# Order of the attention jobs in the last stage of a two-layer decoder step on one Trainium2 core

## The chip, the cores and the metric

The kernel runs on one core of one Trainium2 chip. The metric is the device time of one execution in microseconds (us), as the median of several runs. The engines named below are TensorE (PE, with its weight loads as PEld), VectorE (DVE), ScalarE (ACT), GpSimd (POOL) and SyncE (SP), which only issues transfers here. All data is fp32.

## The reference

One step of a two-layer decoder for a prompt of 1024 rows (eight tiles of 128) and 32 sample rows (8 sequences of 4 tokens with a paged cache of 1024 positions). Only the second layer's attention and what follows matters here.

```
q = rope(rms(heads(q, 8), qn), pos);  k = rope(rms(heads(k, 2), kn), pos)
idx = top_k(sum_h relu(qi . ki) * wi, 256)        # per row, causal
s = q . k[idx] * 128 ** -0.5;  s = where(valid, s, -inf)
yC = (softmax(s) @ v[idx]) * silu(g_c)            # 8 heads, 2 kv heads
y = concat([yC, yX]) @ w_out                      # 1536 x 1024
out = x + y
```

The kernel doesn't gather the 256 keys. An earlier stage turns the selection into a bias for every pair of row and key. The attention then runs densely over the causal keys. A row tile i (0 to 7) so has i + 1 blocks of 128 keys.

## The kernel before

`decoder` runs the first layer, the output projection of the first layer, `layer1_front` (projections and selection of the second layer) and last `layer1_back`, the only function that the change touches.

**Jobs.** In `layer1_back` one job is one row tile and one head: 8 x 8 = 64 jobs. Job g passes through the engines in this way:

- PE `scores(g)` (L4300): q times keys, in one piece of up to 512 columns or two; tiles 4 to 7 ("long") have two pieces, tiles 0 to 3 ("short") have one. The pieces alternate between two banks, and a piece waits until DVE has read the piece two before it.
- DVE `masked(g)` (L4598): adds the bias and takes the maximum of each piece, then forms the negative maximum.
- ACT `exps(g)` (L4476).
- PE `transposes(g)` (L4312), i + 1 blocks of 128x128, and ACT `copies(g)` (L4469) out of PSUM.
- PE `mix(g)` (L4324), i + 1 products with the values, which waits until DVE has read the product of the job before.
- DVE `y_of(g)` (L4615): the product times the reciprocal sum and the gate.

**Slots.** The order of the work on each engine is written out. `back_plan` (L3785) gives 78 slots, and every engine walks them in turn; within a slot it takes the named streams one step each. Engines meet only through semaphores, so an engine can be slots ahead of another. In slot g PE does `transposes(g-3)`, `scores(g)`, `mix(g-4)`; DVE does `masked(g)`, `y_of(g-4)`; ACT does `copies(g-3)`, `exps(g)`. In the first six slots DVE takes a row preparation behind the job, in all others ahead of it.

**Row preparations.** The queries of a tile are loaded, normalised, multiplied by a gain, rotated and transposed ahead of its first job. Tiles 0 and 7 come ready from the stage before. Seven preparations remain, p = 0 to 6: tile 1, the sample rows, then tiles 6, 2, 5, 3, 4. Preparation p starts in slot `START[p]` (L3838): squares on ACT in that slot, sums on DVE in the next, `pow`, gain and rotation on POOL in the three from the next one on (p = 0: on DVE but for the `pow`), transposes on PE `TURN[p]` slots after the start. ACT then copies them over the queries of three tiles before, and waits for that tile's last scores (L4445).

**The samples.** Sixteen units (sequence, half of the cache) need four key pages each, loaded in the slots from 6 on, one unit per slot, unit u in slot u + 4 (unit 2 in slot 6). SP issues the first pages of a unit (L3988) and POOL the last one or two (L4162). PE's `smp_scores(m)` (L4228) in slots 10, 14, 18 and 22 needs the pages of units 4m to 4m + 3. Within a POOL slot the pages stand ahead of the preparation. Value pages and, from slot 37 on, slices of the output weights follow on POOL.

**Ties.** For tiles 5 and 4 a part of the selection is finished on DVE in slots 3 to 18 (`late_ties`, L4634).

**Gates.** Three buffers hold the gates of three tiles. After a tile's last job SP stores the result out of the buffer (`store_y`, five slots behind), and two slots later issues the load of the gate for the tile three further on (`load_gate`, last job + 7), which waits for the store. DVE's `y_of` waits for it (L4621).

**Weights and outputs.** From slot 45 ACT and DVE split the output weights (L4508, L4659), two slices a slot at first, and POOL loads the next slice into one of four buffers when DVE is done with it. From slot 67 PE multiplies by them, nine tiles in a row.

Of the kernel before, what the change touches and what calls it, by code (L numbers as in the profile page):

```python
# [3810 lines left out]
def job_order():  # L3811

    long, short = ([(n, h) for n in of for h in range(QH)] for of in (range(1, TILES, 2), range(0, TILES, 2)))
    return short[0:4] + [job for pair in zip(long, short[4:]) for job in pair] + long[len(short) - 4:]


def layer1_back(nc, c, a, o):
# [9 lines left out]
    rows_in = lambda t: P if t < TILES else SMP  # L3827
    cols_in = lambda t: slice(P * t, P * t + rows_in(t))
    ORDER = job_order()
    nth = lambda g: ORDER[g][0]  # L3830
    head = lambda g: ORDER[g][1]
# [3 lines left out]
    width = lambda g: (block_of(g) + 1) * P  # L3835
    halves = lambda g: [(k, min(512, width(g) - k)) for k in range(0, width(g), 512)]
    first_half = [sum(len(halves(j)) for j in range(g)) for g in range(JOBS + 1)]
    START = [0, 1, 8, 16, 24, 32, 40]  # L3838
    TURN = [7, 8, 9, 9, 9, 9, 9]
    STEPS = [[(p, s - START[p]) for p in range(PREPS) if 0 <= s - START[p] < TURN[p] + 3] for s in range(57)]  # L3840
    TURNED = lambda p: 2 * p + 1 if p else 2
# [862 lines left out]
def decoder(nc, a, o, stop=99):  # L4704
    c = Names()
    with Stage(nc, "all") as st, nc.allow_non_contiguous_dma(reason="columns of a few hundred elements"):
# [53 lines left out]
        with Stage(nc, "odd") as L:  # L4760
            index_memory(c, L)
            layer1_front(nc, c, a, o)
            if stop < 8: return
            layer1_back(nc, c, a, o)
# [57 lines left out]
```

## Time and profile before

| | us |
|---|---|
| median of 3 runs (lowest to highest) | 1782.58 (1781.74 to 1786.09) |
| profiled execution, its own time | 1781.29 |
| its span | 1779.7 |
| PE busy | 1702.0 (96%) |
| DVE busy | 960.0 (54%) |
| ACT busy | 621.0 (35%) |
| POOL busy | 424.9 (24%) |
| mean granted TensorE clock | 0.987 of full |
| stage of the jobs, first scores to last product | about 1400.7 to 1621.7 |

The span is that of the instructions. Around it lie 1.6 us more in the profiled execution. Times inside the stage are counted from the start of the span. A granted clock of 1.00 is 2.4 GHz and 0.50 is 1.2 GHz. The ends of matmuls are modelled, so durations that contain the drain of the array are read with care; a row of the chain of waits shows the part of an instruction after which the next one went on.

### The profile page before, as it was taken

How to read it: one execution, taken by the hardware profiler on the slowest of the kernel's cores; microseconds unless marked ns; L12 is line 12 of the kernel's file. 1: busy time of each engine (PE TensorE's matmuls, PEld its weight loads, DVE VectorE, ACT ScalarE, POOL GpSimd, SP SyncE). 2: the span in 40 equal slices, each digit the busy share in tenths (PEclk: the TensorE clock that was granted, in tenths of full speed). 3: DMA queues.
4: the chain of work that ended last, by engine and by line, in shares of the span. 5: the costliest groups of instructions: out<-in, count | busy, mean ns of one | idle time of the engine just before them, and what ended most of it. 6: DMA issues, size and time to landing. Idle time of an engine off the chain costs nothing. (4 is left out here: it accounts for less than half of the span.)

```text
span 1779.7 us, 26094 instructions
## 1 busy us (share of the span) xinstructions
PE 1702.0 (96%) x9141; PEld 1330.5 (75%) x9141; DVE 960.0 (54%) x2250; ACT 621.0 (35%) x1316; POOL 424.9 (24%) x665
## 2 busy tenths in 40 slices
PE   6999999999999998998999999999999599999999
PEld 5878888777788787886876566888677367777887
DVE  6724744234677665222541568888879575574111
ACT  4322332011122113110220346878856355573100
POOL 5301222100233442000362001121005665520000
PEclk9999999999999999999999999999999699999999
DMA  7433342554566467231333122334544585453231
GB/s 233 137 125 124 115 120 99 160 174 142 177 190 197 128 221 295 81 111 49 103 97 102 43 78 68 103 102 135 165 134 119 187 247 158 131 163 106 85 123 48
DMA packets 145196, 239.18 MB, mean 134 GB/s; under 512 B 21222, under 2 KB 75398, under 8 KB 145066
## 3 DMA queue, kind: packets, MB, share of 16 engines
q1 hardware_dynamic: 120650, 172.75, 30.0%
q0 software_dynamic: 18352, 57.29, 10.3%
q10 hardware_dynamic: 6064, 7.47, 1.2%
q8 instruction: 73, 1.20, 0.3%
q14 instruction: 57, 0.47, 0.1%
HBM read 171.21 MB, written 66.17 MB: 133 GB/s over the span
## 5 line engine op out<-in xcount | busy, mean ns | idle before, releaser
L1292 PE MATMUL ring_acc<-ring_w_hi,layer_xT_hi 128*128 128x512 f32 x640 | 256.6, 401 | 0.2 <-PE all_banks L1438 0.2
L1294 PE MATMUL ring_acc<-ring_w_hi,layer_xT_lo 128*128 128x512 f32 x640 | 249.8, 390 | 0.0
L1293 PE MATMUL ring_acc<-ring_w_lo,layer_xT_hi 128*128 128x512 f32 x640 | 249.7, 390 | 0.0
L2894 PE MATMUL front_acc<-front_w_hi,front_xT_hi 128*128 128x512 f32 x520 | 217.9, 419 | 9.0 <-DVE front_w_lo L3443 5.3
L2896 PE MATMUL front_acc<-front_w_hi,front_xT_lo 128*128 128x512 f32 x520 | 204.8, 394 | 0.0
L2895 PE MATMUL front_acc<-front_w_lo,front_xT_hi 128*128 128x512 f32 x520 | 204.6, 394 | 0.0
L1292 PEld LDWEIGHTS ring_acc<-ring_w_hi,layer_xT_hi 128*128 128x128 f32 x640 | 120.2, 188 | 29.8 <-issue 6.4
L1294 PEld LDWEIGHTS ring_acc<-ring_w_hi,layer_xT_lo 128*128 128x128 f32 x640 | 120.2, 188 | 26.2
L1293 PEld LDWEIGHTS ring_acc<-ring_w_lo,layer_xT_hi 128*128 128x128 f32 x640 | 120.4, 188 | 23.1
L3208 ACT ACTIVATE front_index_rows<-odd_bias,front_candidate,front_minus_sign 128x1024 bf16<-128x1024 f32 (+1 forms) x124 | 132.6, 1075 | 10.5 <-DVE front_candidate L3529 10.5
L2894 PEld LDWEIGHTS front_acc<-front_w_hi,front_xT_hi 128*128 128x128 f32 x520 | 98.2, 189 | 49.6 <-issue 18.1
L2896 PEld LDWEIGHTS front_acc<-front_w_hi,front_xT_lo 128*128 128x128 f32 x520 | 97.7, 188 | 22.5
L2895 PEld LDWEIGHTS front_acc<-front_w_lo,front_xT_hi 128*128 128x128 f32 x520 | 98.3, 189 | 16.0
L1632 ACT ACTIVATE layer_st<-ring_acc 128x512 f32<-128x512 f32 x48 | 28.7, 597 | 226.2 <-PE ring_acc L1294 226.2
L2715 POOL DMA_DIRECT2D all_w<-in_w_odd x57 | 31.9, 560 | 288.3 <-DVE front_w_lo L3443 117.9
L1115 POOL DMA_DIRECT2D all_w<-in_w_even x80 | 44.9, 563 | 216.1 <-DVE ring_w_lo L1860 105.0
L4335 PEld LDWEIGHTS all_banks<-back_v,back_first_scratch 128*128 128x128 f32 x576 | 74.2, 194 | 17.4 <-issue 12.3
L1630 ACT ACTIVATE layer_st<-ring_acc 128x512 f32<-128x512 f32 (+1 forms) x35 | 20.9, 597 | 189.5 <-PE ring_acc L1294 186.1
L4335 PE MATMUL all_banks<-back_v,back_first_scratch 128*128 128x128 f32 x576 | 76.1, 278 | 2.3 <-issue 2.3
L4607 DVE CUSTOM_DVE_ANT_0 back_first_scratch<-back_s,odd_bias 128x512 f32<-128x512 f32 (+3 forms) x96 | 51.3, 557 | 48.3 <-PE back_s L4309 47.7
L4479 ACT ACTIVATE back_first_scratch<-back_first_scratch 128x1024 f32<-128x1024 f32 (+4 forms) x64 | 49.8, 779 | 65.0 <-DVE back_first_scratch L4613 45.4
L4321 PE MATMUL all_banks<-all_ident,back_first_scratch 128*128 128x128 f32 x288 | 44.7, 283 | 8.5 <-ACT back_first_scratch L4474 5.4
(726 smaller groups left out, 3576.1 us busy)
## 6 DMA issues: line engine op xcount, KB each, us to landing
all_w<-in_w_even POOLq DMA_DIRECT2D x80, 256.0 KB, 3.9
h_even<-layer_st SPq DMA_DIRECT2D x79, 256.0 KB, 2.1
all_w<-in_w_odd POOLq DMA_DIRECT2D x61, 256.0 KB, 3.5
h_odd<-front_st SPq DMA_DIRECT2D x55, 256.0 KB, 2.1
layer_scratch<-h_even SPq DMA_DIRECT2D x46, 256.0 KB, 3.0
all_scratch<-in_w_mem SPq DMA_DIRECT2D x32, 256.0 KB, 3.2
all_scratch<-h_even SPq DMA_DIRECT2D x32, 256.0 KB, 3.6
all_scratch<-x SPq DMA_DIRECT2D x14, 512.0 KB, 3.7
```

The source lines that it names most:

```text
L1115: pool.dma_start(raw[n % RAW][:, :], a["w_even"][ORDER[chunk][0] // CW, :, CW * kk:CW * kk + CW]).then_inc(w_in[n % RAW], 16)
L1292: T.matmul(out[0:rows, :], xh[:, kk, to], wh[:, r, :], start=(kk == 0), stop=False)
L1293: T.matmul(out[0:rows, :], xh[:, kk, to], wl[:, r, :], start=False, stop=False)
L1294: ins = T.matmul(out[0:rows, :], xl[:, kk, to], wh[:, r, :], start=False, stop=(kk == KC - 1))
L2894: T.matmul(out[0:rows, :], xh[:, k, to], wh[:, r, :], start=(k == 0), stop=False, skip_group_check=True)
L2895: T.matmul(out[0:rows, :], xh[:, k, to], wl[:, r, :], start=False, stop=False, skip_group_check=True)
L2896: ins = T.matmul(out[0:rows, :], xl[:, k, to], wh[:, r, :], start=False, stop=(k == KC - 1), skip_group_check=True)
L3208: A(flags_at(i), rows_at(i), ACT.Sign, bias=cand[:, j:j + 1], scale=minus[:, j:j + 1] if k else -1.0, accum_out=cnt[:, j:j + 1]).then_inc( ...
L4321: ins = T.transpose(psT[:, 512 * j + P * q:512 * j + P * q + P], sm[g % 3][:, P * (k + q):P * (k + q) + P], c.ident[:, :])
L4335: ins = T.matmul(bankO[:, 0:P], pT[g % 2][:, k, :], v[:, k, HD * (h // 4):HD * (h // 4) + HD], start=(k == 0), stop=(k == i))
L4479: A(y, y, ACT.Exp, bias=neg[g % 3][:, :], scale=SC, accum_out=tot[g % 5][:, :]).then_inc(ex, 1)
L4607: V.tensor_tensor_reduce(sm[u][:, k:k + n], psS[:, 512 * (m % 2):512 * (m % 2) + n], c.bias[:, bias_at(i) + k:bias_at(i) + k + n], 1.0, -3 ...
```

## The change

The order of the jobs and the slots in which preparations start are changed. No instruction is added or removed.

```diff
 def job_order():
     long, short = ([(n, h) for n in of for h in range(QH)] for of in (range(1, TILES, 2), range(0, TILES, 2)))
-    return short[0:4] + [job for pair in zip(long, short[4:]) for job in pair] + long[len(short) - 4:]
+    return [job for pair in zip(short, long) for job in pair]
@@ layer1_back
-    START = [0, 1, 8, 16, 24, 32, 40]
+    START = [0, 1, 6, 14, 22, 30, 38]
     TURN = [7, 8, 9, 9, 9, 9, 9]
```

Before, jobs 0 to 3 are short, then long and short take turns from job 4 (long) to job 59 (short), and jobs 60 to 63 are long. After, even jobs are short and odd jobs long. First and last job of each tile:

| tile | 0 | 7 | 1 | 6 | 2 | 5 | 3 | 4 |
|---|---|---|---|---|---|---|---|---|
| before | 0, 11 | 4, 18 | 13, 27 | 20, 34 | 29, 43 | 36, 50 | 45, 59 | 52, 63 |
| after | 0, 14 | 1, 15 | 16, 30 | 17, 31 | 32, 46 | 33, 47 | 48, 62 | 49, 63 |

So short jobs but for the first come later, by up to three slots, and long ones earlier by three (the last four by three to none). Everything that hangs on a tile's last job (stores, gate loads) moves with it. Preparations 2 to 6 move two slots ahead on all engines and on SP, with their loads (the load for p + 2 goes out two slots behind p's transposes). The slots of the sample work, ties, weights and outputs stay.

## Rows read from the trace of the kernel before

**Rows 1.** The page: the whole span, and PE and its clock in 40 slices.
```profile
PE   6999999999999998998999999999999599999999
PEclk9999999999999999999999999999999699999999
```

**Rows 2.** By stretch: length, PE, PEld, DVE, ACT, POOL busy, granted clock, DMA share, GB/s.
```profile
1400.60:1449.00 48.40, 35.62 (x174) 23.57 (x174) 35.50 (x98) 23.67 (x70) 31.34 (x40) 0.76 0.88 270
1449.00:1476.00 27.00, 26.57 (x185) 19.51 (x189) 16.89 (x59) 14.72 (x32) 16.68 (x20) 1.00 0.77 229
1559.00:1578.00 19.00, 16.83 (x112) 13.45 (x111) 13.93 (x46) 13.30 (x29) 3.94 (x8) 1.00 0.45 145
1578.00:1612.00 34.00, 34.00 (x230) 27.54 (x229) 26.45 (x94) 26.41 (x61) 6.86 (x13) 1.00 0.54 170
```

**Rows 3.** The chain of waits from 1380 to 1450: start, us, what.
```profile
1400.01 4.39 DMA all_scratch<-h_odd
1405.51 1.23 DVE back_first_scratch L4541
1407.09 1.66 POOL back_first_scratch L4143
1410.08 1.48 DVE back_first_scratch L4541
1416.64 2.10 DVE back_first_smp L3774
1421.52 2.07 PE back_s L4309 x2
...
1436.24 1.72 PE back_s L4309 x4
1437.96 1.78 PE all_banks L4335 x16
1439.75 0.87 PE all_banks L4321 x8
```

**Rows 4.** DVE in order of time: start, us, line, operation, output and inputs.
```profile
1411.70 0.29 DVE L4607 CUSTOM_DVE_ANT_0 back_first_scratch<-back_s,odd_bias 128x128 f32<-128x128 f32 x1
...
1414.42 0.69 DVE L4607 CUSTOM_DVE_ANT_0 back_first_scratch<-back_s,odd_bias 128x512 f32<-128x512 f32 x1
...
1415.76 0.42 DVE L4613 SCALAR_TENSOR_TENSOR back_first_scratch<-back_first_scratch 128x1 f32<-128x1 f32 x1
```

**Rows 5.** PE in order of time, with its idle time and releaser in brackets.
```profile
1409.96 4.17 PE L4309 MATMUL back_s<-keys_kT,back_qT 128*128 128x512 f32 x4
...
1449.00 1.93 PE L4239 MATMUL back_x<-back_first_smp 128*32 128x512 f32 x16 [1.66 <-issue]
...
1475.90 1.92 PE L4239 MATMUL back_x<-back_first_smp 128*32 128x512 f32 x16 [0.43 <-issue]
```

**Rows 6.** POOL in order of time.
```profile
1426.30 0.79 POOL L4162 DMA_DIRECT2D back_first_smp<-in_cache_attn_kT  x1 [2.02 <-issue]
1427.49 0.73 POOL L4162 DMA_DIRECT2D back_first_smp<-in_cache_attn_kT  x1 [0.40 <-issue]
...
1433.70 1.66 POOL L4143 TENSOR_TENSOR back_first_scratch<-back_first_scratch,all_half 128x8 f32<-128x8 f32 x1 [0.89 <-DVE back_first_scratch L4542]
1435.43 2.15 POOL L4147 TENSOR_TENSOR all_scratch<-all_scratch,back_first_scratch 128x1024 f32<-128x1024 f32 x1
...
1440.68 2.37 POOL L4153 TENSOR_TENSOR all_scratch<-all_scratch 128x1024 f32<-128x1024 f32 x1
1444.25 0.74 POOL L4162 DMA_DIRECT2D back_first_smp<-in_cache_attn_kT  x1 [1.20 <-issue]
1445.02 0.47 POOL L3774 TENSOR_TENSOR all_scratch<-all_scratch 128x128 f32<-128x128 f32 x1
```

**Rows 7.** PE by stretch: length, PE busy, granted clock, DMA share, GB/s.
```profile
1381.00:1384.00 3.00, 0.21 (x1) 0.89 0.00 0
1384.00:1387.00 3.00, 2.90 (x11) 0.50 0.33 104
1387.00:1390.00 3.00, 3.00 (x8) 0.50 0.82 274
...
1447.00:1449.00 2.00, 0.34 (x4) 1.00 0.92 278
1449.00:1456.00 7.00, 7.00 (x49) 1.00 0.78 225
```

**Rows 8.** All gate loads (L3979), of their own line: time from issue to landing.
```profile
DMA to landing us min/median/max: 3.6/5.3/8.4
```

**Rows 9.** SP's own waits, 1384 to 1640: line, releaser, us in total, times, longest.
```profile
SPq L3979 <- DMA y_odd<-all_mem_vals: 4.7, 1, 4.7
```

## The prediction, made before the kernel was run

> **What bounds the kernel.** I read the page first: PE is busy in nine tenths of nearly every slice, and only slice 31 of 40 falls to 5 with the clock at 6 [rows 1]. That slice is where the changed stage begins. Busy time by stretch then divides the stage [rows 2]. From 1400.6 to 1449.0 PE is busy 35.6 of 48.4 us at a mean clock of 0.76. After that it is full but for small holes (26.6 of 27.0 us; 34.0 of 34.0 at the end) and one of 2.2 us between 1559 and 1578. So the stage is a start-up that something else bounds, and then a stretch that only the sum of PE's work bounds. The change leaves that sum alone. It can gain only by doing more PE work inside the start-up, and lose by new holes behind it.
>
> The chain of waits says what bounds the start-up [rows 3]: the load of the query rows, the sums on DVE, the `pow` on POOL, DVE again for the sample rows' sums, and the rotation that DVE makes for tile 1 (it begins at 1416.6 and ends at 1421.0). Behind it stands `masked(5)`, which releases the second piece of `scores(6)` at 1421.5. From there PE is on the chain.
>
> **Part 1, the order: what is done by slot 14.** At full clock the chain gives a long job of 8 blocks 1.72 us of scores, 1.78 of products and 0.87 of transposes [rows 3], so 0.215, 0.22 and 0.11 us a block. By the start of slot 14 the new order has done 63 blocks of scores in place of 50, 46 of transposes for 39, 45 of products for 31: 13 x 0.215 + 7 x 0.11 + 14 x 0.22 = 6.7 us more work. Before, PE stood at that point at 1447.3 (1449.0 less the idle 1.66) [rows 5]. Were all of it to fit into idle time, the gain would be 6.7 us; if none did, zero.
>
> How much fits follows from DVE. A short `masked` costs about 0.4 us and a long one 2 x 0.69 and the maximum, some 1.6 us [rows 4]. Up to slot 5 the new order has three long ones in place of one, 2.4 us more. Job 1 is now long: its scores run at the low clock, where a piece of 512 columns takes 1.0 us per record, 2.0 us a piece [rows 5], so DVE is free of it at about 1407.0, and the sums that started at 1405.5 [rows 3] start then. The whole chain of the preparation is 1.6 us late. Job 3 costs 1.2 us more, and the rotation ends near 1423.0 instead of 1421.0. But PE no longer waits for that: scores 3 and 4, the transposes of job 1 (released near 1412 by ACT) and `scores(5)` stand before it, and I find PE busy without a break from about 1417.5. It takes the product of job 1 (3.5 us at the low clock) until 1425.0. Summing slots 6 to 13 from there, with the first transposes at a mixed clock, three preparation transposes (0.6, 0.5, 0.7) and the first sample scores (1.9), I come to slot 14 at 1449.8. That is 2.5 us later with 6.7 us more done: **-4.2 us**. Bounds: -6.7 and 0.
>
> **Part 2, preparation 2 before the pages.** This costs. POOL issued its pages of units 2 to 5 first, then `pow` and gain product, then the two pages of unit 6, the second product, unit 7's page at 1444.25 and the rotation behind it [rows 6]. Unit 7's page is what `smp_scores(1)` waited for in slot 14: 4.75 us from the issue to 1449.0, 1.66 of it a hole [rows 5, 6]. Two slots ahead, all three steps of the preparation stand before unit 6. POOL's first page goes out 1.65 us later (the sample rows' `pow` hangs on the late DVE chain): 1427.9. From there, three pages at 1.15 spacing to 1431.1, `pow` and product to 1435.1, two pages behind a switch of 1.2 us to 1438.2, product to 1440.6, switch and a page to 1442.5, rotation (six of 0.45) to 1445.2, two pages, and unit 7's page at 1448.8. With the same 4.75 us the scores start at 1453.5, against PE's arrival at 1449.8: a hole of 3.7 us in place of 1.7, **+2.0 us**. Bounds: -1.7 (the page lands in time) and +3.
>
> The third preparation's steps likewise move from slots 17 to 19 to slots 15 to 17, so its rotation (2.7 us) now stands ahead of the pages of units 14 and 15, which `smp_scores(3)` needs in slot 22; that wait was 0.43 us [rows 5]. The same count puts unit 15's page at 1476.6 and its landing 3.7 us later at 1480.3, with PE there at 1478.4: a hole of 1.9, **+1.5 us**. Bounds: -0.4 and +3.
>
> **Part 3, the gates.** Tile 6's gate is issued in slot 21 and read by `y_of(17)` in slot 21; before, it was issued in slot 18 and read in slot 24. The same holds for tile 5 (slot 37) and tile 4 (slot 53). The buffer's store goes out behind `y_of(14)`; a gate load waited 4.7 us for such a store [rows 9], and lands 3.6 to 8.4 us after issue, 5.3 at the median [rows 8]. So the gate is there about 10 us after the last `y_of` of the old tile, and is wanted three slots, 8.4 us, later (19, 20 and 21 at 3.5, 1.6 and 3.3): DVE stands 1.6 us, with `masked(22)` queued behind it. PE waits for it only at `mix(18)`, behind the sample scores of slot 22, transposes and scores: 3.1 us of cover. Around slot 37 the three slots hold sample products too and last some 11 us: no stall. In slot 53 they last about 7.4 us and PE's cover is 1.4 us (transposes and scores of 5 blocks): 1.2 us at worst. I take **+0.4 us**, bounds 0 and +6.
>
> **Part 4, the weights' hole** [rows 2]. It follows from the sample rows' stores and the round of DVE, POOL, load and ACT per weight slice, tied to slots 44 to 50. There the pairs of jobs have 9 blocks in place of 10, so each pair of slots hides 0.55 us less: three pairs, less than half of them inside the hole, **+0.6 us**, bounds 0 and +1.7. The queries' copies on ACT that move two slots (each 0.6 us) stay; each now waits for scores of one slot before, not of six, and ACT's own `exps` has already waited for those: nothing. The last four long jobs become two and two; by then PE is full: **0**, bounds -0.5 and +0.3.
>
> **Sum.** -4.2 + 2.0 + 1.5 + 0.4 + 0.6 = +0.3. The profiled execution's 1781.3 becomes 1781.6; the median of the runs lay 1.3 us above it, so **1783 us**. Differences under 0.3% (5.3 us) are what a measurement of this kernel can't tell from none.
>
> **Rival 1: the pages don't hold PE.** Part 2 rests on one delay of 4.75 us from POOL's issue, in a stretch in which the DMA engines are 0.88 busy [rows 2]. If the load is lighter there or PE comes later to slot 14 than I think, the holes shrink while the gain stays: -4.2 - 1.7 - 0.4 + 1.0, so about 1777.3. For it: most pages of a unit go out on SP, whose queue the change leaves as it is. Against: the order on POOL is fixed, and 7 us of work have moved before the page.
>
> **Rival 2: the hole costs the clock too.** PE stood still for some 3 us before 1384, and the next 6 us ran at 0.50; a stop of 1.66 us at 1447 left it at 1.00 [rows 7]. The hole of 3.7 us is past the first. Six us at half clock lose 3.0 us, and PE then comes to slot 22 late enough to find its pages (-1.5): 1784.5.
> The Trainium skill (TensorE: Matmul & The Clock Gate, What's actually happening) says that the throttled state is the default and that activity lifts it; by that the loss would come with any long enough stop, and it is this rival's 1784.5 and not 1783. The rows agree in both directions.
>
> **Rival 3, slower: the gates.** If loads land as late as the slowest row, 8.4 us [rows 8], the gate comes some 13 us after the last `y_of` of the old tile. DVE then stands 4.7 us in slot 21, 2 in slot 37 and 5.7 in slot 53, and PE less its cover: 1.6 + 0 + 4.3 = 5.9 us, and two stops of DVE that long cost clock as well. It decides once landing exceeds about 7 us. Time: 1789 us. Against: the median is 5.3, and the slow rows are from the crowded start.
>
> **Chances.** The balance above 0.46; rival 1 0.20; rival 2 0.22; rival 3 0.12. Rival 1 straddles the bound: just over half of it is faster by more than 5.3 us, and nearly all of rival 3, with a little of rival 2, is slower by more. Faster 0.12, same 0.75, slower 0.13. Range 1777.5 to 1788.5: it leaves out the ends of rivals 1 and 3.
>
> **What would show it.** PE busy without a break from about 1417.5 instead of 1421.5 (part 1); POOL's `pow` of tile 6 ahead of its pages of unit 4, and PE's idle before the second sample scores near 3.7 us, with the clock behind it (part 2, rival 2); a DVE wait for a gate load in slots 21 and 53 where there was none (part 3); a weights' hole of 2.5 to 3 us. I am wrong if the first scores of job 5 come later than 1419, or if the second sample scores start without a wait.

## The result, and the profile after

The changed kernel took 1796.2 us (median; 1789.9 to 1803.2), the kernel before 1782.2 us beside it (1780.3 to 1786.1): a ratio of 1.0063, 95% interval 1.0049 to 1.0078, about 11 us slower. The medians lie 14 us apart. The runs of the changed kernel scatter by 13 us; I go by the ratio and its interval. The forecast was no change, 1783 us, and a range that ended at 1788.5. It was wrong in sign and in size.

| profiled execution, us | before | after |
|---|---|---|
| span | 1779.7 | 1795.4 |
| first scores of the changed stage | 1400.68 | 1402.44 |
| second sample scores (slot 14) | 1449.00 | 1453.10 |
| fourth sample scores (slot 22) | 1475.90 | 1482.33 |
| last sample product (slot 44) | 1557.69 | 1571.00 |
| first transposes behind the jobs (L4361) | 1621.63 | 1637.33 |

The stage itself starts between 1400.5 and 1404.8 in all profiled executions here, with either order, so the first 1.8 us are no effect of the change. From the first scores to L4361 the work is the same: 220.95 us before, 234.89 after, 13.9 us more. Behind L4361 the two agree.

The page after, PE and its clock in 40 slices, answers to [rows 1]: the slice in which the stage starts reads 6 in place of 5, and behind it two slices read 8 where before had 9.

```profile
PE   6999999999999998998999999999999698989999
PEclk9999999999999999999999999999999798999999
```

By stretch (as in [rows 2]), the start-up of the changed kernel:

```profile
1402.40:1417.50 15.10, 9.58 (x25) 4.74 (x25) 9.68 (x23) 7.44 (x15) 6.83 (x13) 0.73 1.00 303
1417.50:1440.00 22.50, 19.70 (x109) 13.66 (x113) 19.20 (x48) 10.66 (x39) 18.29 (x17) 0.84 0.87 261
1440.00:1453.10 13.10, 12.17 (x84) 8.59 (x84) 10.08 (x33) 8.61 (x19) 8.41 (x14) 1.00 0.84 240
```

PE in order of time, changed kernel, answers to [rows 5]; the holes are in brackets:

```profile
1417.77 0.45 PE L4321 MATMUL all_banks<-all_ident,back_first_scratch 128*128 128x128 f32 x1 [1.43 <-ACT back_first_scratch L4474]
...
1428.01 0.30 PE L4321 MATMUL all_banks<-all_ident,back_first_scratch 128*128 128x128 f32 x1 [1.71 <-ACT back_first_scratch L4474]
1453.10 1.92 PE L4239 MATMUL back_x<-back_first_smp 128*32 128x512 f32 x16 [0.93 <-issue]
...
1482.33 3.12 PE L4239 MATMUL back_x<-back_first_smp 128*32 128x512 f32 x16 [3.59 <-issue]
1502.74 0.41 PE L4321 MATMUL all_banks<-all_ident,back_first_scratch 128*128 128x128 f32 x2 [2.41 <-ACT back_first_scratch L4474]
1505.84 1.65 PE L4309 MATMUL back_s<-keys_kT,back_first_scratch 128*128 128x384 f32 x2 [1.35 <-DVE back_first_scratch L4607]
...
1585.76 0.52 PE L4321 MATMUL all_banks<-all_ident,back_first_scratch 128*128 128x128 f32 x3 [1.11 <-ACT back_first_scratch L4474]
1603.95 2.05 PE L4335 MATMUL all_banks<-back_v,back_first_scratch 128*128 128x128 f32 x8 [3.87 <-issue]
```

The hole that the forecast put at 3.7 us before the second sample scores is 0.93. The one before the fourth, put at 1.9, is 3.59. Two more follow in slots 24 to 26, and one of 3.87 in slot 53. The clock was low behind the pair of slots 24 to 26 (0.50 from 1505 to 1510), and behind these two:

```profile
1478.60:1482.30 3.70, 0.15 (x2) 1.00 0.99 351
1482.30:1487.00 4.70, 4.67 (x25) 0.64 0.92 256
...
1600.00:1604.00 4.00, 0.13 (x2) 0.80 1.02 238
1604.00:1608.00 4.00, 4.00 (x14) 0.50 0.82 301
```

(Length, PE busy, granted clock, DMA share, GB/s; changed kernel.) At 0.50 PE stands at 1.2 GHz, the lower of its levels.

**A ledger by stretch.** To compare kernels whose orders differ, I credit the new order with the work that it has done earlier: 6.7 us by slot 14, 5.1 by slot 22, 2.9 by slot 44, none at L4361 (an estimate from the prices per block in [rows 3]). What remains is time lost (+) or won (-) against the profile of before, counted from each execution's own first scores:

| kernel | start to slot 14 | 14 to 22 | 22 to 44 | 44 to L4361 | sum |
|---|---|---|---|---|---|
| changed | -4.4 | +3.9 | +9.1 | +5.3 | +13.9 |
| order_only | -7.3 | +1.8 | +4.2 | +5.0 | +3.7 |
| starts_only | +1.9 | +3.4 | +7.0 | -0.9 | +11.5 |
| prep3_late | -4.7 | +0.1 | +4.6 | +4.0 | +4.0 |
| loads_behind_gate | -3.9 | +4.2 | +5.9 | +0.2 | +6.3 |
| order_tail | -7.3 | +1.5 | +3.9 | +1.1 | -0.8 |
| starts_4_to_6 | -0.3 | +0.3 | +5.7 | +0.4 | +6.0 |
| prep4_early | +0.4 | -0.5 | +6.0 | +0.3 | +6.3 |
| prep4_late | -4.5 | +4.0 | +5.0 | +3.0 | +7.5 |
| tail_start | -7.0 | +1.8 | +4.2 | +3.6 | +2.5 |

Each row is one execution. How far two executions of the same instructions lie apart can be read off the table: `changed` and `loads_behind_gate` run the same instructions up to slot 53, and have +9.1 and +5.9 between slots 22 and 44; `changed`, `prep3_late` and `prep4_late` have the same tail, and +5.3, +4.0 and +3.0 there. Up to slot 22 such rows agree within 0.8 us. A difference of less than 3 us behind slot 22 therefore says little. The sums agree with the ratios of the runs within 3 us, but for `loads_behind_gate` (+6.3 against 11).

### The profile page after: what moved, and what is told of

Same layout as the page of the kernel before. It is cut to its first block and busy times, and to the rows that moved or that the text cites. A ratio compares the mean times of both kernels' runs of the same rounds, so it can differ in the third digit from the quotient of the medians.

```text
span 1795.4 us, 26095 instructions
## 1 busy us (share of the span) xinstructions
PE 1706.3 (95%) x9141; PEld 1331.7 (74%) x9141; DVE 969.5 (54%) x2250; ACT 622.2 (35%) x1316; POOL 426.2 (24%) x665
## 5 line engine op out<-in xcount | busy, mean ns | idle before, releaser
L4607 DVE CUSTOM_DVE_ANT_0 back_first_scratch<-back_s,odd_bias 128x512 f32<-128x512 f32 (+3 forms) x96 | 51.5, 556 | 46.1 <-PE back_s L4309 45.3
L4479 ACT ACTIVATE back_first_scratch<-back_first_scratch 128x128 f32<-128x128 f32 (+3 forms) x64 | 49.6, 775 | 74.8 <-DVE back_first_scratch L4613 51.7
```

The source lines that it names most:

```text
L4479: A(y, y, ACT.Exp, bias=neg[g % 3][:, :], scale=SC, accum_out=tot[g % 5][:, :]).then_inc(ex, 1)
L4607: V.tensor_tensor_reduce(sm[u][:, k:k + n], psS[:, 512 * (m % 2):512 * (m % 2) + n], c.bias[:, bias_at(i) + k:bias_at(i) + k + n], 1.0, -3 ...
```

## The experiments

Each was timed beside the kernel before, whose median was 1784.5, 1784.4 and 1783.5 us in the three sets.

**order_only and starts_only: the two halves of the change, each alone.**

```
order_only:   the new job_order()   START = [0, 1, 8, 16, 24, 32, 40]
starts_only:  the old job_order()   START = [0, 1, 6, 14, 22, 30, 38]
```

> The new order of jobs with the old starts of the preparations (0, 1, 8, 16, 24, 32, 40). Theory A (the page of unit 15 is late in slot 22 because preparation 3 stands ahead of it on GpSimd): TensorE's idle of 3.6 us before the fourth sample scores falls under 1 us, and with it the low clock behind it; the stage is some 6 us shorter than with the whole change, about 1789 us. Theory B (the gates of tiles 6, 5 and 4 alone cost the time): the hole in slot 22 stays and the time stays near 1796. Under both the stop of about 4 us at the first product of tile 4 (slot 53) stays. The transposes for tile 6 now come in slot 17, the slot of its first scores, which may cost 1 us.

> The old order of jobs with the new starts (0, 1, 6, 14, 22, 30, 38). Theory A: sample pages late in slots 14 and 22, TensorE idle 2 to 4 us in slot 22 with the clock at its lower level behind it, 1786 to 1790 us. Theory B: the gates are as before, so the time is that of before, 1782 us.

order_only: 1788.9 us, ratio 1.0021 (1.0009 to 1.0033). starts_only: 1795.0 us, 1.0054 (1.0037 to 1.0072). Most of the loss is the earlier starts; the order alone wins 7.3 us by slot 14 and has given it back, and more, by the end. In order_only the hole before the fourth sample scores is 0.49 us, as theory A had it. In starts_only the late page shows in slot 14 and not in slot 22, where the hole is 0.35:

```profile
1454.01 3.11 PE L4239 MATMUL back_x<-back_first_smp 128*32 128x512 f32 x16 [3.14 <-issue]
```

Behind it the clock stood at 0.57 for 4 us. Where the order alone loses late shows in PE's time of order_only:

```profile
1579.53 1.70 PE L4309 MATMUL back_s<-keys_kT,back_qT 128*128 128x512 f32 x4 [2.49 <-ACT back_qT L4446]
...
1597.66 1.13 PE L4335 MATMUL all_banks<-back_v,back_first_scratch 128*128 128x128 f32 x8 [1.99 <-issue]
```

The first is `scores(49)`, whose queries come from preparation 6: in the new order the last tile's jobs begin earlier, and a preparation that starts in slot 40 is too late for them. The second is the wait for a gate; both theories had it at about 4 us, and it is 1.99.

**prep3_late: the changed kernel with preparation 3 behind the pages of unit 15.**

```
START = [0, 1, 6, 18, 22, 30, 38]
```

> The whole change, but preparation 3 (tile 2, first wanted in slot 32) starts in slot 18 and not 14, so that its three steps on GpSimd stand behind all key pages. Theory A: unit 15's page goes out some 7 us earlier, the hole of 3.6 us in slot 22 is gone, the clock stays at its upper level there, and the sample rows' softmax behind it no longer stops TensorE for 2.4 and 1.4 us: 1787 us. Rival (the softmax stops TensorE because job 23 is now a long one ahead of it on ScalarE): the hole in slot 22 goes, those in slots 24 and 25 stay, 1791 us.

1789.4 us, 1.0032 (1.0020 to 1.0045). Slot 14 to 22 falls from +3.9 to +0.1; PE finds the pages of slot 22 there without a wait, and the clock is 1.00 up to 1495. So with this order the page hole of slot 22 is preparation 3's. The stops beside the sample rows' softmax stay, at 2.81 and 1.71 us, as the rival had it: they are not the late page's work. POOL of the changed kernel shows how (compare [rows 6]):

```profile
1474.20 0.74 POOL L4162 DMA_DIRECT2D back_first_smp<-in_cache_attn_kT  x1 [1.70 <-issue]
1475.35 0.72 POOL L4162 DMA_DIRECT2D back_first_smp<-in_cache_attn_kT  x1 [0.41 <-issue]
1477.14 0.72 POOL L4162 DMA_DIRECT2D back_first_smp<-in_cache_attn_kT  x1 [1.07 <-issue]
```

The last is unit 15's page. It goes out at 1477.14. The stage began 1.8 us later than before, so this is 1475.4 by the forecast's count, which had 1476.6. PE stands from 1478.7 (1477.0 by that count, forecast 1478.4). The scores start 5.2 us after the issue, not 3.7.

**loads_behind_gate: SyncE holds the later rows' loads until the gate of tile 4 is in.**

```
             for _ in range(19):
                 yield
+            sp.wait_ge(g_in[7 % 3], 16 * 3)
             for j in range(2):
                 load_y(j)
                 load_x(j)
```

> The whole change, and SyncE waits for tile 4's gate before it issues the first loads of the output stage (y and x rows, 1.6 MB), which it had issued 0.4 us behind the gate's load. Theory C (the gate is late because those loads share the DMA engines with it): it lands 4 to 5 us after its issue and not 8, DVE's wait of 4.8 us falls to about 1.5, TensorE's stop of 3.9 us with the low clock behind it goes, 1791 us against 1796. Rival (the gate is late because its store goes out late): the gate is issued at the same point and lands as late, no change.

1793.5 us, 1.0064 (1.0039 to 1.0089); its profiled execution took 1788.0. The times don't tell it from the changed kernel, so what follows rests on the traces. SyncE's queue in the changed kernel:

```profile
1591.74 0.35 SPq L3983 DMA_DIRECT2D y_odd<-all_mem_vals  x1
...
1595.36 0.32 SPq L3979 DMA_DIRECT2D all_mem_vals<-h_odd  x1
1595.80 0.51 SPq L4088 DMA_DIRECT2D all_scratch<-y_odd  x1
1596.35 0.42 SPq L4094 DMA_DIRECT2D all_scratch<-x  x1
1597.11 0.34 SPq L4088 DMA_DIRECT2D all_scratch<-y_odd  x1
1597.50 0.97 SPq L4094 DMA_DIRECT2D all_scratch<-x  x1
```

The gate of tile 4 waits for the store of its buffer, and four loads of 1.6 MB together follow within 2.2 us. VectorE reads it 8.1 us after its issue, and its other two waits of this kind are for tiles 6 and 5 (slots 21 and 37); the kernel before had none:

```profile
1479.66 0.35 DVE L4623 SCALAR_TENSOR_TENSOR all_mem_keysT<-all_banks,back_first_scratch,all_mem_keysT 128x128 f32<-128x128 f32 x1 [1.47 <-DMA all_mem_keysT<-h_odd]
1551.57 0.35 DVE L4623 SCALAR_TENSOR_TENSOR back_gate<-all_banks,back_first_scratch,back_gate 128x128 f32<-128x128 f32 x1 [1.81 <-DMA back_gate<-h_odd]
1603.50 0.35 DVE L4623 SCALAR_TENSOR_TENSOR all_mem_vals<-all_banks,back_first_scratch,all_mem_vals 128x128 f32<-128x128 f32 x1 [4.78 <-DMA all_mem_vals<-h_odd]
```

With the loads held back, VectorE reads the gate 5.9 us after its issue (theory C: 4 to 5), the last wait is 2.27 us, PE's hole 1.37, and slot 44 to L4361 falls from +5.3 to +0.2. The other kernels with the new order bear the hole out: 3.60 us in prep3_late and 2.54 in prep4_late without the wait, 1.62 in order_tail with it.

**order_tail: the new order, old starts but preparation 6 in slot 38, and the loads held back.**

```
START = [0, 1, 8, 16, 24, 32, 38]   and the wait of loads_behind_gate
```

> The new order with the old starts, but the last preparation (tile 4) two slots ahead, and SyncE waits for tile 4's gate before it issues the first loads of the output stage. With the new order and the old starts alone the stretch from the last sample product to the first transpose of the output stage took 66.1 us against 63.9 before, with stops of 2.5 us at scores(49) (its queries copied in its own slot) and 2.0 us at the first product of tile 4. If these two are the cause of that loss the stretch falls to some 62 us and the time to 1785 us, that of before. If the loss comes from the even pairs of jobs in the weight slots, it stays at 65 and the time at 1788 us.

1782.1 us, 0.9990 (0.9979 to 1.0000): the best version here, and not measurably better than before. `scores(49)` no longer waits, and from the last sample product to L4361 it takes 62.2 us, as expected if the two stops were the cause. At the gate PE stands

```profile
1591.79 1.13 PE L4336 MATMUL all_banks<-back_v,back_first_scratch 128*128 128x128 f32 x8 [1.62 <-ACT back_first_scratch L4475]
```

**samples_later and all_mended: does the sample stream's place against long and short slots matter?** The new order swaps which slots are long.

```
samples_later:  new order, old START,  for s in range(6, 45) -> range(7, 46)  (the "smp" stream)
all_mended:     START = [0, 1, 8, 18, 24, 32, 38], the gate's wait, and the same shift
```

> The new order with the old starts, and the whole stream of sample steps one slot later (7 to 45 for 6 to 44), so that the samples' softmax meets a long job in the slots in which it did before. Parity theory (the softmax on ScalarE and VectorE is covered by a long job's scores and products only if the long ones are the even ones): from the fourth sample scores to the transposes of the samples' weights 19 us as before, not 21, no stop of 1.5 us there, 1787 us. Rival (the clock that falls behind the 32 small products makes that stretch long whatever stands beside it): 21 us again, no gain.

> The new order with every cost that was named taken out at once: starts 0, 1, 8, 18, 24, 32, 38, SyncE's loads behind the gate, sample steps one slot later. If the causes named add up, the stage keeps the 4 us that the start-up gains: 1781 us against 1784 for before. If each only moves a wait to the next place, it is 1785 or more.

1802.8 us, 1.0109 (1.0094 to 1.0125), and 1793.1 us, 1.0057 (1.0044 to 1.0069). Both lost. The pages of unit 7 now fell behind preparation 2 after all: PE stood 3.72 us before 1452.74 in the one and 3.63 us before 1454.91 in the other. The clock behind it was 1.00 in samples_later and 0.50 in all_mended. From the fourth sample scores to the first L4267 it took 22.8 and 21.3 us, no less than the rival had. Since this hole mixes in, the question they were made for isn't answered by them. What they show is that the stream can't be moved one slot later. The profile of samples_later is of its fastest execution (1795.3 us), so a part of its loss is in no trace.

**starts_4_to_6 and prep4_early: preparations 4 to 6 early, and preparation 4 alone, in the old order.**

```
starts_4_to_6:  START = [0, 1, 8, 16, 22, 30, 38]
prep4_early:    START = [0, 1, 8, 16, 22, 32, 40]
```

> The old order; of the preparations only 4, 5 and 6 start two slots ahead, 2 and 3 as before. Theory A (the loss of 10 us by the starts alone comes from preparations 2 and 3, which stand ahead of key pages on GpSimd): the time of before, 1784 us, or 1 us less. Rival (the shift costs on every preparation, through ScalarE's squares and copies): 1788 us or more.

> The order of before; only preparation 4 begins two slots early (22), preparations 5 and 6 as before (32, 40). Theory (POOL's preparation steps beside VectorE's softmax of the sample rows): the loss of starts_4_to_6 is made in slots 22 to 26. From the fourth sample scores to the first L4267 it takes 22 to 24 us in place of 18.9, the start-up up to slot 22 stays (smp3 at 75.2 us after the first scores), and the ratio is 1.002 to 1.003 (+3 to +5 us). Rival (preparations 5 and 6, and their gates, made the loss): this stretch stays within 19.5 us and the ratio is 0.999 to 1.001.

1788.8 us, 1.0026 (1.0016 to 1.0036), and 1789.9 us, 1.0029 (1.0015 to 1.0042). Preparation 4 alone makes the whole loss of the three: the ledger has +5.7 and +6.0 between slots 22 and 44, and nothing elsewhere. The stretch up to the first L4267 takes 23.9 us in prep4_early, inside the 22 to 24 of the theory. (The rival of starts_4_to_6 had the right time, but not the cause: preparations 5 and 6 cost nothing.) POOL's steps moved beside VectorE's work on the sample rows' softmax. In prep4_early, POOL, DVE and PE:

```profile
1493.23 1.90 POOL L4147 TENSOR_TENSOR all_scratch<-all_scratch,back_first_scratch 128x1024 f32<-128x1024 f32 x1
...
1498.34 2.35 POOL L4153 TENSOR_TENSOR all_scratch<-all_scratch 128x1024 f32<-128x1024 f32 x1
```
```profile
1493.86 1.82 DVE L4576 TENSOR_SCALAR back_first_smp<-back_first_smp,back_first_scratch 128x1028 f32<-128x1028 f32 x1
1495.83 0.75 DVE L4576 TENSOR_SCALAR back_first_smp<-back_first_smp,back_first_scratch 128x1028 f32<-128x1028 f32 x1
1497.94 2.77 DVE L4613 SCALAR_TENSOR_TENSOR back_first_scratch<-back_first_scratch 128x1 f32<-128x1 f32 x1
1500.82 0.35 DVE L4623 SCALAR_TENSOR_TENSOR all_mem_keysT<-all_banks,back_first_scratch,all_mem_keysT 128x128 f32<-128x128 f32 x1
```
```profile
1497.58 1.19 PE L4309 MATMUL back_s<-keys_kT,back_first_smp 128*128 128x256 f32 x2 [2.33 <-DVE back_first_scratch L4607]
1501.27 1.20 PE L4335 MATMUL all_banks<-back_v,back_first_scratch 128*128 128x128 f32 x4 [2.50 <-issue]
```

VectorE's L4613 handles one number a partition and takes 0.22 us at the median. Here it takes 2.77 and ends at 1500.71, as POOL's L4153 ends (1500.69). The first L4576 takes 1.82 us, and the second 0.75 where POOL runs nothing. PE stands twice: 2.33 us for scores whose bank VectorE reads late (L4607, queued behind the slow L4576), and 2.50 us for a product that has to wait until VectorE has read the one before (L4623, queued behind the slow L4613; it ends 0.10 us before PE starts). ScalarE's `exps` stands for L4613 too, 6.86 us, but PE's product started before it was done. In the kernel before, the same pair ran clear of POOL's steps:

```profile
1490.45 0.76 DVE L4576 TENSOR_SCALAR back_first_smp<-back_first_smp,back_first_scratch 128x1028 f32<-128x1028 f32 x1
1491.35 0.77 DVE L4576 TENSOR_SCALAR back_first_smp<-back_first_smp,back_first_scratch 128x1028 f32<-128x1028 f32 x1
1493.49 0.22 DVE L4613 SCALAR_TENSOR_TENSOR back_first_scratch<-back_first_scratch 128x1 f32<-128x1 f32 x1
```

The Trainium skill (SBUF — State Buffer, SBUF: two separate sides) says that VectorE and GpSimd share a pair of ports that one of them holds for a whole instruction while the other stands fully blocked, and that a VectorE operation with two SBUF inputs meets it against a GpSimd operation that reads SBUF. L4613 has two tensor inputs in SBUF and L4153 reads SBUF, and the two ends 0.02 us apart are what that rule gives. It isn't one chance meeting. Of the 416 records of this line in the 13 traces (32 long jobs each) 55 took over 0.3 us, and every one ends 0.01 to 0.03 us behind a POOL operation, also in the kernel before:

```profile
1553.97 1.27 DVE L4613 SCALAR_TENSOR_TENSOR back_first_scratch<-back_first_scratch 128x1 f32<-128x1 f32 x1
```

(L4153 ends there at 1555.23.) Such meetings are thus nothing new; what counts is whether PE has work in hand while VectorE stands. Two things the rule doesn't settle here. By the stamps L4613 began 0.40 us before L4153, so the trace doesn't show POOL holding the ports first. And L4576 has one tensor input, which isn't the case named; the trace shows it slow beside POOL, not why.

**prep4_late: the changed kernel with preparation 4 back in slot 24.**

```
START = [0, 1, 6, 14, 24, 30, 38]
```

> The changed kernel with preparation 4 at slot 24, where before had it; preparations 2, 3, 5 and 6 stay early. Theory (preparation 4 is a cost of its own): the hole of 3.6 us before the fourth sample scores stays, the stretch from there to the first L4267 falls from 27.9 us to 21 to 24, and the ratio from 1.0063 to 1.003 to 1.005. Rival (the hole in slot 22 and the low clock behind it are the whole loss, preparation 4 adds nothing): the stretch stays at 26 us or more and the ratio at 1.006.

1791.6 us, 1.0042 (1.0028 to 1.0056). From the fourth sample scores to the first L4267 it takes 20.2 us in place of 27.9, a little below what the theory named; before it was 18.9. By the ratios preparation 4 would cost 4 us in the changed kernel, but the two intervals overlap. About the clock this run said something unasked:

```profile
1478.70:1482.50 3.80, 0.24 (x3) 1.00 1.04 395
1482.50:1487.00 4.50, 4.46 (x38) 1.00 0.89 279
```

Its hole of slot 22 is 3.59 us, the same as in the changed kernel to the hundredth, and the clock stayed at 1.00 behind it, where the changed kernel's fell to 0.64. The mean clock of the whole stretch was 0.69 in the changed kernel and 0.92 here, and `loads_behind_gate`, which runs the changed kernel's instructions up to there, had 0.79 and took 24.4 us. PE's idle time in it was 3.8, 2.1 and 3.7 us. So of the 7.7 us some 1.6 are stops and the rest is clock. What belongs to preparation 4 is the stop before the second piece of a long job's scores: 1.35, 1.52 and 1.71 us in the three kernels that have it early in the new order, and under 0.3 in the four that have it in slot 24 with the sample stream in its place. In the changed kernel VectorE reads the bank late because an operation ahead of it in the queue met POOL's L4153 (1501.39 to 1503.74):

```profile
1501.87 2.44 DVE L4576 TENSOR_SCALAR back_first_smp<-back_first_smp,back_first_scratch 128x1028 f32<-128x1028 f32 x1
```

In loads_behind_gate it was the short operation behind the second of these, on 128x32, with 2.63 us in place of 0.19.

**tail_start: order_tail without the held loads.**

```
START = [0, 1, 8, 16, 24, 32, 38]
```

> The new order with the old starts but for preparation 6, which begins at slot 38; the loads of the later rows are not held behind the gate of tile 4. Theory (order_only lost its time to preparation 6, which in the new order begins too late for the jobs that read it, and the holding back of the loads adds little): ratio 0.999 to 1.001, and the hole of 2.5 us at scores(49) of order_only is gone. Rival (the held loads made order_tail fast): ratio 1.002 as order_only, with a hole of over 2 us between slots 48 and 54.

1785.9 us, 1.0008 (0.9994 to 1.0021). The hole at `scores(49)` is gone, so it was preparation 6's start. The gate's is back, and with it the clock (0.63 behind it):

```profile
1593.98 2.05 PE L4335 MATMUL all_banks<-back_v,back_first_scratch 128*128 128x128 f32 x8 [3.38 <-issue]
```

The ledger puts the held loads at 2.5 us (+3.6 against +1.1); the intervals of the two ratios just overlap, so the runs alone don't show that holding them helps.

## Why the prediction was wrong

Up to slot 22 the forecast said -4.2 + 2.0 + 1.5 = -0.7 us, and the changed kernel's ledger says -0.4. That is luck; the terms were off and cancelled. Behind slot 22 it said +1.0, and the ledger says +14.4. This is the step that failed: the stretch behind the start-up was taken as full whatever moves in it ("by then PE is full: **0**"), so the sum had no term for what the order and the early preparations do to VectorE, ScalarE and the clock there, and a term of 0.4 for the gates. Slots 22 to 44 cost 9.1 us and the tail 5.3. Neither of the two signs of being wrong that I had named came: the first scores of job 5 stood at 1418.0, before 1419, and the second sample scores did wait.

**Part 1, the fill (-4.2).** Right in sign, too small: with preparation 2 in its old place the new order wins 7.0 to 7.3 us by slot 14, slightly past the bound of -6.7. The picture of PE "without a break from about 1417.5" was wrong: holes of 0.83, 1.71 and 0.93 us stand between it and slot 14.

**Part 2, preparation 2 (+2.0).** The size of the cost was about right (order_only -7.3, changed -4.4: 2.9 us) and its place wrong. The page hole is 0.93 us. By the forecast's count (1.8 us less, for the later start of the stage) unit 7's page goes out at 1447.4, not 1448.8, PE arrives at 1450.4, not 1449.8, and the scores start 4.0 us after the issue, not 4.75: 2.8 us in all, which is the hole that is missing. In the old order, starts_only, it is there, 3.14 us with the clock of rival 2 behind it. In the changed kernel the page hole is a third of the cost. The rest fits what I left out, the preparation's work on ScalarE and the clock behind it. ScalarE in the changed kernel:

```profile
1426.32 1.06 ACT L4418 ACTIVATE back_first_smp<-all_scratch 128x1024 f32<-128x1024 f32 x1 [0.20 <-issue]
1427.29 1.06 ACT L4474 ACTIVATE back_first_scratch<-all_banks 128x512 f32<-128x512 f32 x2
```

and in order_only, and PE behind it there:

```profile
1427.97 1.08 ACT L4474 ACTIVATE back_first_scratch<-all_banks 128x512 f32<-128x512 f32 x2 [0.45 <-issue]
```
```profile
1428.71 0.30 PE L4321 MATMUL all_banks<-all_ident,back_first_scratch 128*128 128x128 f32 x1 [1.02 <-ACT back_first_scratch L4474]
```

The early preparation puts its squares (L4418) ahead of the copy that PE waits for. PE stands 1.71 us instead of 1.02, and then ran at 0.57 to 1432, where order_only ran at 1.00. It is so in every kernel with the new order: 1.71 to 1.92 us and 0.57 to 0.60 behind it in the four with preparation 2 in slot 6, 0.74 to 1.02 us and 1.00 in the five with it in slot 8. I had followed POOL's queue alone, and the rule that every moved instruction counts was mine to apply to ACT as well.

**Part 2, preparation 3 (+1.5).** The mechanism was right, the size was not: 3.9 against prep3_late's 0.1. The issue came 1.2 us earlier than forecast and PE 1.4 us; the landing took 5.2 us and not 3.7, in a stretch with the DMA engines full (share 0.99). Of rival 2, the clock fell here in two executions of three that had this hole (0.64 in the changed kernel and 0.63 in loads_behind_gate, 1.00 in prep4_late), and in the changed kernel not in slot 14 where I had put it.

**Preparation 4: no term at all.** Edits to preparations 4 to 6 were priced only through gates and weights. In the old order preparation 4 alone costs 6.0 us in the ledger and 1.0029 by the runs, and two long VectorE operations beside POOL's account for PE's stops there. Neither the sum nor a rival had this. How much of it the changed kernel pays stays open: 4.1 us by prep4_late, of which most is clock; hardly anything by prep3_late, which has preparation 4 early too, at +4.6 between slots 22 and 44 against order_only's +4.2. The stop of 1.35 to 1.71 us is there in each.

**Part 3, the gates (+0.4).** The waits came where they were named, of 1.5 us in slot 21 (forecast 1.6), 1.8 in slot 37 (none) and 4.8 in slot 53 (2.6, of which 1.2 was to reach PE). Rival 3 had 5.7 us there for VectorE and 4.3 for PE; PE stood 3.87. I took the median landing for a load that shares the DMA engines with four others, though the row with the spread was in hand. With the clock it is some 2.5 to 5 us (5.1 by loads_behind_gate, 2.5 by tail_start against order_tail).

**Part 4 (+0.6).** The weights' hole shrank: 1.11 us where before had 2.17 in three pieces. "By then PE is full: 0" was wrong: with the order alone, 4.2 us go between slots 22 and 44. About half is holes of 0.2 to 1.5 us (PE idle 2.7 us in place of 0.8), and half is clock (mean 0.96 in place of 0.98 over 84 us), while long and short jobs stand in other slots against the sample stream and the preparations. Which of them makes each of these holes stays open; samples_later and all_mended, which were to tell it apart, had a new hole of their own.

**The sum again**, for the changed kernel: fill -7.3, preparation 2 +2.9, slots 14 to 22 +3.9 (order_only lost 1.8 there with preparation 3 in its old place, prep3_late 0.1), slots 22 to 44 +4.2 as in order_only and +4.9 more, the tail +5.3: -7.3 + 2.9 + 3.9 + 4.2 + 4.9 + 5.3 = 13.9 us. Of the +4.9, 3.2 us is what this execution lost against `loads_behind_gate` with the same instructions, in clock; the other 1.7 fits preparation 4's stop. The ratio of the runs says 11.

## What to carry to other kernels

A stage that looks like "PE full but for small holes" may have its streams interleaved with almost no slack, as this one had, so a start moved by two slots has to be followed on every engine it uses, not on the queue that looks crowded. List which VectorE operations would run beside GpSimd's large SBUF operations before and after a move, above all the tiny ones that another engine waits for. Read a load's landing from its neighbours in the queue at that moment, and carry its slow end through to the engine that bounds the stage.

## What the runs showed that was not expected

- A VectorE operation on 128x1 took 2.77 us beside a GpSimd operation on 128x1024, against 0.22 at the median, and ended 0.02 us behind it. So did, within 0.03 us, all 55 slow records of that line in 13 traces.
- The same stop of PE, 3.59 us, left the granted clock at 1.00 in one kernel and at 0.64 in another. Elsewhere 3.72 us left it at 1.00 (samples_later), and 2.54 us (prep4_late, slot 53, 0.66), 3.14 us (starts_only, 0.57) and 3.87 us (changed, 0.50) cost it; 1.66 us in before cost nothing [rows 7]. A stop of 2.5 to 4 us is a risk to the clock here, not a fixed price.
- Two executions of the same instructions lay 3.2 us apart between slots 22 and 44, by their clocks (0.90 and 0.94 over the stretch). A ledger from one trace each can't price a cause smaller than that.
- Two changes that lose time apart or together (the order 1.0021, the starts 1.0054) hide one that is even: the order with one start moved by two slots and one wait added is at 0.9990.
